# Two-layer transformer block on one core: VectorE adds the squares of the second layer's norms, and one modulation block moves to the first FFN step

## The reference, cut to what matters

```python
def _rmsnorm(x, g):
    xf = x.astype(jnp.float32)
    y = xf * lax.rsqrt(jnp.mean(xf * xf, axis=-1, keepdims=True) + EPS)
    return (y * g.astype(jnp.float32)).astype(x.dtype)

def _modulation(cvec, w_mod, b_mod):
    h = jax.nn.silu(cvec) @ w_mod + b_mod
    shift, scale, gate = jnp.split(h[:, None, :], 3, axis=-1)
    return shift, scale, gate

def _pre(x, g, shift, scale):
    return _rmsnorm(x, g) * (1 + scale) + shift

# second_block, layer 1 (odd), behind the even layer's output product:
sh, sc, gt = _modulation(c, o_w_mod[i], o_b_mod[i])
sh_c, sc_c, gt_c = _modulation(c_ctx2, o_w_mod[i], o_b_mod[i])
cb_c, cc_c, cx_c, cg_c, q_c, k_c, v_c, ag_c = _odd_proj(_pre(xc, o_norm[i], sh_c, sc_c), o_w_in[i])
cb, cc, cx, cg, q, k, v, ag = _odd_proj(_pre(x, o_norm[i], sh, sc), o_w_in[i])
```

## Time and profile before

| | before |
|---|---|
| median of 3 runs | 763.36 us (762.36 to 763.48) |
| profiled execution | 761.49 us, span 759.4 us |
| PE busy | 745.4 us, 98% |
| PEld busy | 680.0 us, 90% |
| DVE busy | 647.7 us, 85% |
| ACT busy | 382.8 us, 50% |
| DMA | 205 GB/s in the mean |
| chain that ended last | PE 93%, DVE 4%, DMA 2%, ACT 1% |

### The profile page before, as it was taken

How to read it: one execution, slowest core, us unless ns; L and a number is a source line. 1 busy time by engine, 2 the same in 40 slices (tenths; PEclk the granted TensorE clock), 3 DMA queues, 4 the chain that set the end, 5 groups by cost and what they waited for, 6 DMA issues and landing times.

```text
span 759.4 us, 12749 instructions
## 1 busy us (share of the span) xinstructions
PE 745.4 (98%) x5276; PEld 680.0 (90%) x5276; DVE 647.7 (85%) x1038; ACT 382.8 (50%) x526; POOL 1.3 (0%) x10
## 2 busy tenths in 40 slices
PE   8899999999999999999999999999999999999996
PEld 4689899999989999999999988888777899999995
DVE  5868888797998999999988999999989977788653
ACT  4264465568366555454465541322464345555652
POOL 0000000000000000000000000000000000000000
PEclk9999999999999999999999999999999999999998
DMA  9989999866564666766754262222106542575101
GB/s 366 417 335 375 391 384 345 301 222 224 216 222 174 253 240 222 243 255 230 258 179 167 84 250 72 95 79 88 56 0 242 207 144 98 174 275 218 57 1 55
DMA packets 23642, 155.98 MB, mean 205 GB/s; under 512 B 2678, under 2 KB 4255, under 8 KB 5152
## 3 DMA queue, kind: packets, MB, share of 16 engines
q1 hardware_dynamic: 21404, 150.37, 53.3%
q10 hardware_dynamic: 2182, 4.82, 2.0%
HBM read 154.11 MB, written 1.07 MB: 204 GB/s over the span
## 4 chain that ended last, share of the span: by engine, by line
PE 93%; DVE 4%; DMA 2%; ACT 1%; issue 0%; DVEq 0%; SPq 0%
PE psum L1518 78%; PE psum L1609 2%; DMA arena<-in_w 2%; DVE w_lo L889 1%; PE psum L1852 1%; PE psum L2025 1%; PE psum L2049 1%; PE psum L2037 1%; PE psum L1838 1%; PE psum L1702 1%; PE psum L1557 1%; DVE w_lo L922 1%; PE psum L1586 0%; PE psum L1687 0%; PE psum L1657 0%; PE psum L1910 0%
## 5 line engine op out<-in xcount | busy, mean ns | idle before, releaser
L1518 PE MATMUL psum<-h_hi,w_hi 128*128 128x256 f32 (+1 forms) x1280 | 386.9, 302 | 1.5 <-DVE h_lo L1314 0.5
L1518 PE MATMUL psum<-h_lo,w_hi 128*128 128x256 f32 (+1 forms) x1280 | 382.5, 299 | 0.0
L1518 PE MATMUL psum<-h_hi,w_lo 128*128 128x256 f32 (+1 forms) x1280 | 382.4, 299 | 0.0
L1518 PEld LDWEIGHTS psum<-h_hi,w_hi 128*128 128x128 f32 x1280 | 244.5, 191 | 12.5 <-issue 2.6
L1518 PEld LDWEIGHTS psum<-h_lo,w_hi 128*128 128x128 f32 x1280 | 244.6, 191 | 8.0 <-issue 0.5
L1518 PEld LDWEIGHTS psum<-h_hi,w_lo 128*128 128x128 f32 x1280 | 244.5, 191 | 7.6
L922 DVE TENSOR_TENSOR w_lo<-raw,w_hi 128x2048 fp32r<-128x2048 f32 x90 | 206.0, 2288 | 29.6 <-ACT w_hi L396 28.7
L396 ACT CAST w_hi<-raw 128x2048 fp32r<-128x2048 f32 x90 | 171.3, 1906 | 39.8 <-DMA raw<-in_w 30.8
L889 DVE SCALAR_TENSOR_TENSOR w_lo<-raw,cond 128x1024 fp32r<-128x1024 f32 x88 | 104.2, 1221 | 0.8
L889 DVE SCALAR_TENSOR_TENSOR w_lo<-raw,arena 128x1024 fp32r<-128x1024 f32 x48 | 56.8, 1220 | 11.3 <-DMA raw<-in_w 5.6
L614 ACT ACTIVATE arena<-psum,vec 128x256 f32<-128x256 f32 x44 | 22.5, 564 | 58.6 <-DVE g_lo L1160 54.2
(11 more groups left out here) (242 smaller groups left out, 719.4 us busy)
## 6 DMA issues: line engine op xcount, KB each, us to landing
raw<-in_w SPq DMA_DIRECT2D x138, 1024.0 KB, 4.9
arena<-in_w SPq DMA_DIRECT2D x3, 1024.0 KB, 14.7
xs<-in_xs SPq DMA_DIRECT2D x1, 1024.0 KB, 9.0
consts<-diff ACTq DMA_DIRECT2D x8, 128.0 KB, 7.2
cond<-diff ACTq DMA_DIRECT2D x1, 1024.0 KB, 13.9
xs<-in_xs ACTq DMA_DIRECT2D x1, 1024.0 KB, 8.4
out<-xs SPq DMA_DIRECT2D x2, 384.0 KB, 2.5
consts<-in_c ACTq DMA_DIRECT2D x1, 512.0 KB, 3.9
```

Source lines behind the costliest of these rows:

```text
L1518: last = mm(out, w[a], x[b], start=start and n == 0, stop=stop and n == 2, skip_group_check=skip)
```

## The change

- In the order of loads, one modulation block stands ahead of the down chunk of FFN step 0 (chunk 32), and one instead of two ahead of chunk 76 (`LIN_EOUT + 4`). Between the two places each block is used one place earlier.
- VectorE adds the squares of the first four tiles of x (a 512-wide and a 256-wide addition, behind the evacuation of the second output chunk) and signals `odd_x_added`. It adds the three sums of context pairs to one with two more additions.
- TensorE makes the sums for x (tiles 0 and 4 to 7, five instead of eight) behind the third quarter of the last output chunk, and then one for the context instead of three.
- The last two context sums move into `staggered`, ahead of its last 24 matmuls, and ScalarE's inverse root for the context moves between its two copies of q.

```diff
--- before.py
+++ after.py
@@ -80,11 +80,11 @@
         order += [("mod", m + k) for k in range(n)] + [("lin", j)]
         m += n
     for j in range(LIN_FFN + 1, LIN_EIN):
-        n = int(j in [ffn_down(c) for c in range(1, FF_STEPS - 3)] + [ffn_up(0) + 2])
+        n = int(j in [ffn_down(c) for c in range(FF_STEPS - 3)] + [ffn_up(0) + 2])
         order += [("mod", m + k) for k in range(n)] + [("lin", j)]
         m += n
     for j in range(LIN_EIN, N_LIN):
-        n = 2 if j == LIN_EOUT + 4 else int(j in (LIN_EIN + 2, LIN_EIN + 3) or LIN_EOUT < j < LIN_EOUT + 4 or LIN_OIN + 7 <= j < LIN_OIN + 11)
+        n = int(j in (LIN_EIN + 2, LIN_EIN + 3) or LIN_EOUT < j <= LIN_EOUT + 4 or LIN_OIN + 7 <= j < LIN_OIN + 11)
         order += [("mod", m + k) for k in range(n)]
         m += n
         order += [("lin", j)]
@@ -783,7 +783,8 @@
             for i in range(2):
                 act.wait_ge(sem("lin_done"), LIN_OPEN + LIN_OIN + i + 1)
                 nc.scalar.copy(q_raw[:, 512 * i:512 * (i + 1)], wide[:, i, :]).then_inc(sem("q_raw"), 1)
-            rstd_of("odd_ctx")
+                if i == 0:
+                    rstd_of("odd_ctx")
             shift_hi("odd_ctx")
 
             act.wait_ge(sem("k_done"), 1)
@@ -1360,8 +1361,14 @@
                     for t in range(2):
                         for s in range(2):
                             eout_evac(i, t, s)
+                if i == 1:
+                    dve.wait_ge(sem("sq_odd_x"), 4)
+                    me.mark(nc.vector.tensor_tensor(norm_tmp[:, 0:2, :], norm_tmp[:, 0:2, :], norm_tmp[:, 2:4, :], ALU.add))
+                    me.wait()
+                    nc.vector.tensor_tensor(norm_tmp[:, 0, :], norm_tmp[:, 0, :], norm_tmp[:, 1, :],
+                                            ALU.add).then_inc(sem("odd_x_added"), 1)
                 if i == 2:
-                    split(LIN_OIN, done=2)
+                    split(LIN_OIN, done=1)
                     mod_bias(36, 44)
                     coefficients(32, "o_norm", mod_row(O_SC, 0))
                     coefficients(40, "o_norm", mod_row(O_SC, 1))
@@ -1371,6 +1378,10 @@
             for k in (0, 2, 4):
                 dve.wait_ge(sem("sq_odd_ctx"), k + 2)
                 nc.vector.tensor_tensor(gain_sq[:, k, :], gain_sq[:, k, :], gain_sq[:, k + 1, :],
+                                        ALU.add).then_inc(sem("odd_ctx_added"), 1)
+            for k in (2, 4):
+                dve.wait_ge(sem("odd_ctx_added"), 2 + k // 2)
+                nc.vector.tensor_tensor(gain_sq[:, 0, :], gain_sq[:, 0, :], gain_sq[:, k, :],
                                         ALU.add).then_inc(sem("odd_ctx_added"), 1)
             split(LIN_OIN + 1)
             norm("odd_x", 7)
@@ -1560,7 +1571,7 @@
                     if k == end:
                         last.then_inc(sem("sumsq"), 1)
 
-            def staggered(j, first, second, ready):
+            def staggered(j, first, second, ready, between=None):
 
                 pe.wait_ge(sem("lo_done"), j + 2 - AS_LOADED)
                 for k in range(KT):
@@ -1571,6 +1582,8 @@
                                           k == KT - 1, skip=True)
                             if k == KT - 1 and n == 0 and m == 1:
                                 last.then_inc(sem("lin_done"), 1)
+                if between:
+                    between()
                 for k in range(KT):
                     last = triple(second[1], whl((j + 1) % SPL, 256 * k + P, P), hhl(k, 0, T), k == 0, k == KT - 1)
                 last.then_inc(sem("lin_done"), 1)
@@ -1943,16 +1956,15 @@
                         last = triple(wide[:, 2 + m, s * T:(s + 1) * T], whl(j % SPL, 256 * k + P * m, P),
                                       hhl(hk, s * T, T), n == 0, n == KT - 1)
                     last.then_inc(sem("eout_x" if s == 0 else "lin_done" if m else "eout_ctx"), 1)
-                    if s == 0 and m == 0:
-                        sum_squares("odd_x", range(6))
                     if s == 1 and m == 0:
-                        sum_squares("odd_x", (6, 7))
-                        pe.wait_ge(sem("odd_ctx_added"), 3)
-                        sum_squares("odd_ctx", (0, 2, 4))
+                        pe.wait_ge(sem("odd_x_added"), 1)
+                        sum_squares("odd_x", (0, 4, 5, 6, 7))
+                        pe.wait_ge(sem("odd_ctx_added"), 5)
+                        sum_squares("odd_ctx", (0,))
 
             pe.wait_ge(sem("eout_evac"), 12)
-            staggered(LIN_OIN, halves(wide[:, 0, :]), halves(wide[:, 1, :]), tile_ready("odd_x"))
-            sum_squares("odd_ctx", (6, 7))
+            staggered(LIN_OIN, halves(wide[:, 0, :]), halves(wide[:, 1, :]), tile_ready("odd_x"),
+                      lambda: sum_squares("odd_ctx", (6, 7)))
 
             j = LIN_OIN + 2
             pe.wait_ge(sem("lo_done"), j + 1 - AS_LOADED)
```

## The result

The changed kernel takes 765.55 us (median of 12 runs, 764.05 to 767.13). The kernel before took 762.35 us beside it (12 runs, 761.52 to 765.52). The ratio is 1.0037 with a 95% interval of 1.0028 to 1.0046, that is 2.8 us slower (2.1 to 3.5). The forecast was 765.7, with a difference of 2.35 us. Part of how close the two totals are is luck: the base was 763.36 in the three runs known then and is 762.35 here, so the base was 1.0 us too high. By the ratio the difference is 2.8 us and the forecast 0.45 too small; by the two medians it is 3.2 us and the forecast 0.85 too small.

The account below looks back on a forecast made before the run. The prediction took TensorE, with 93% of the chain, to bound the kernel. From a median of 763.36 us, +3.6 (modulation) +0.9 (clock) -2.15 (sums) gave 765.7 us, range 763.9 to 767.5.

Parts of the forecast that it names:

- What bounds the kernel: Whole chain: TensorE carries 93%, so work taken off it and waits it newly meets count in full.
- The sums, -2.15 us: Last output chunk: ten passes of column sums leave TensorE at 0.216 us each, gaining 2.15 us.
- What VectorE gets there, and what hides it: Last output chunk: VectorE's added additions cost nothing; cover 2 us before the context sums, 0.6 us before the norm.
- rival D: Last output chunk: new waits cost about 1 us more, total 765.8 to 766.7 us; chance 0.08.
- The modulation, +3.6 us: FFN: first down-projection 3.0 us late, eighth 3.54, taken as 3.6 with restarts; nothing returned later.
- Rival C: First down-projection: VectorE's idle time covers the modulation, only the sums count, 761.2 us; chance 0.07.
- The clock, +0.9 us net: New FFN pause: TensorE's clock falls, costing 1.5 us, of which about 0.6 is absorbed.
- A: The forecast itself: sums, modulation and a clock fall in the new FFN pause, 765.7 us; chance 0.50.
- B: New FFN pause: the clock stays up, only sums and modulation count, 764.8 us; chance 0.32.

Follow-up runs that it names:

- e1: Kernel before with only the modulation moved to the first FFN step, sums of squares as before: 766.94 us, ratio 1.0054.
- e3: Changed kernel with 13 matmuls on zeros in TensorE's new pause ahead of the first down-projection: 764.47 us, ratio 1.0019.
- e7: Kernel before, with VectorE adding all eight context squares behind the split of chunk 78, one context sum on TensorE instead of five: 761.11 us, ratio 0.9980.
- e8: As e7, plus one VectorE addition for x (six sums instead of eight) and small bias and coefficient instructions moved later: 760.95 us, ratio 0.9971.
- e5: Changed kernel with the moved modulation block halved, its context part left out (a probe that computes less): 762.00 us, ratio 0.9989.
- e2: Changed kernel with the modulation put back where it was, only the sums changed: 766.25 us, ratio 1.0039.
- e0: Changed kernel run once more, unchanged: 765.17 us, ratio 1.0030.

## Why the prediction was right, point by point

**What bounds the kernel.** It held. What TensorE waited newly or did less is found in the end of the stretch: 3.64 less 2.14 is its 1.50.

**The sums, -2.15 us.** Rest went from 282.56 to 280.42, -2.14, and from 282.63 (e1) to 280.48 (e3), -2.15. The cost of a pass, 0.216 us, needed no correction.

**What VectorE gets there, and what hides it.** Both covers were there, of the sizes worked out. VectorE and ScalarE in the changed kernel:

```profile
606.45 1.66 DVE L1349 SCALAR_TENSOR_TENSOR xs<-psum,modv,xs 128x256 f32<-128x256 f32 x4 [0.80 <-PE psum L1529]
...
612.60 1.09 DVE L1380 TENSOR_TENSOR arena<-arena 128x256 f32<-128x256 f32 x3
613.73 0.88 DVE L1384 TENSOR_TENSOR arena<-arena 128x256 f32<-128x256 f32 x2
...
617.24 0.47 ACT L421 ACTIVATE rstd<-psum,small 128x256 f32<-128x256 f32 x1 [4.10 <-PE psum L1568]
...
619.39 0.48 DVE L963 SCALAR_TENSOR_TENSOR h_lo<-att,modv,h_hi 128x256 fp32r<-128x256 f32 x1
```

VectorE now waits for TensorE at the third output chunk (0.80 us idle) where it was late before. The five additions end at 613.73 + 0.88 = 614.61; TensorE asks for them behind ten passes, near 617.1 (the root that these ten release starts at 617.24): cover 2.5 us, predicted 2. The first low part ends at 619.87, and TensorE starts chunk 76 behind its 24 matmuls and a restart at 620.34: cover 0.47 us, predicted 0.6. TensorE meets no new wait there, so rival D is false. The cover is thin all the same: e7 and e8, which shorten the sums further, are through it by 0.2 us.

**The modulation, +3.6 us.** d0 came 3.08 us late (predicted 3.0), d7 3.64 (predicted 3.54, with the restart 3.6), and +3.61 in e1. From d0 to d7 the down-projections are 121.54 / 7 = 17.36 us apart, as forecast. The wait has just the form that was named: modulation, split, `g_lo`, one new wait of 2.92 us ahead of the first down-projection. Rival C, a cover on VectorE, is false. What does hide work is shown by e5: about 1.1 us of idle time ahead of this one split, not a share of the whole. The Trainium skill (Perfetto Trace Analysis, Identifying the Most-Contended Engine) ranks engines by their occupancy; that work on an engine with room is free is the prediction's reading of it, the page doesn't say so. Read that way it is contradicted by the trace, with 3.6 us for 4.8 us of work.

**The clock, +0.9 us net.** It is A in some executions and B in others. Gross 1.48 (predicted 1.5), net 0.98 at the eighth step (predicted 0.9), in the one execution where a fall is traced; 0.7 by the medians of the times, 1.4 by those of the spans. The Trainium skill (TensorE: Matmul & The Clock Gate, Part 1) states that activity releases the throttled state; the trace agrees as far as it goes: TensorE works without a break from the fall, near 250.4 us, until the clock is back at 1.00, near 253.9. That the estimate was so near is chance: it took the price to be twice what the delay of another fall would cost, and no row carried that. The argument for B, that a pause of 2.0 us passed without a fall, was one execution's luck: at the same place near 22 us, seven of twelve profiled executions have a fall behind pauses of 1.28 to 1.96 us, and five have none behind pauses of 1.07 to 2.00.

**The size that was off.** The sum was 2.35, measured 2.8 (2.1 to 3.5), and 2.3 (1.6 to 3.0) when repeated. The terms as the runs give them are 1.50 and 0.7 to 1.4, thus 2.2 to 2.9. Both measurements hold that, and the forecast. One bound of the prediction doesn't follow from its own terms: a clock term of up to 4.5 us, 0.6 of it absorbed, takes A to 764.8 + 3.9 = 768.7 us, not 767.9. Whether the first measurement has something over the sum stays open. The waits at line 1692 could be part of it: none in the two profiled executions of the kernel before, 1.2 and 0.4 us in those of the kernel after. The measured differences of e3 (1.4 us by the ratio against 1.53) and e5 (-0.8 against -0.83) speak against a lasting share, for these have that wait too, and their time follows the table.

**What the base hid.** The prediction took 763.36 us from three runs and a profile of 761.49. The median of 32 runs beside later kernels is 762.72, and the profiled execution had the least c28 of all. To take the change as a difference was right; to put it on the median of three made an error of 1.0 us in the total, and by chance that made up for the 0.85 us by which the difference of the medians was missed.

## What to carry to other kernels

Work moved onto an engine with idle time is free only up to the idle time that lies ahead of the next hand-over to the bounding engine; measure that cover at the place (1.2 us of the 4.8 here) and count everything above it in full, for a loop between two engines of nearly equal period gave nothing back here. If a change shortens the bounding engine's work, look at which work it had been covering: e2 lost 3 us of the sums' gain to a wait that the old sums had hidden, and e8 got nearly its whole gain by placing the additions where nobody on TensorE waited behind them and moving the modulation nowhere. Price a new pause on TensorE by its length and by a possible clock fall, and compare two profiles from a common point, since one transfer-fed stretch here differs by up to 1.7 us between executions. Don't infer from one execution without a fall of the clock that a pause is harmless.

## What the hardware did that was not expected

- The granted clock fell after the pause and not in it: at 1.00 until TensorE was back at work at 249.88 us, then 0.50 from about 250.5 to 253.9. The end of the trace before had the fall about 1.7 us behind the last matmul. So the whole low stretch hit work, and none of it the pause.
- One and the same pause, 2.92 and 2.93 us long, gave a fall in one profiled execution (e0) and none in two others (after, e1).
- Shorter pauses were followed by a fall too: near 22 us, where TensorE waits for transfers, seven of twelve profiled executions have one, behind pauses of 1.28 to 1.96 us. What it costs there no run shows; in the 84 runs of the kernel before, the mean clock and the time don't go together.
- 13 matmuls on zeros in the pause, on a TensorE that had nothing else to do, went with a mean clock that never was under 0.996 in 11 runs (0.993 to 0.997 without), for about 0.7 us of gain in the time (765.17 to 764.47, uncertain by 1.0).
- Not all of a fall's price stays. Behind the first down-projection, with waits for VectorE at the later steps, 1.48 us became 0.98 in the trace. Ahead of TensorE's last quarters, with nothing to take it up, filling the pause gave 1.8 us, uncertain by 1.3; that fits, but doesn't show it.
